# An rwkv chunk scan on one core: products half crossed and half straight over TensorE's four quadrants, in alternation; the chain of a unit spread over three steps, both directions in one eviction, the state carried in PSUM

## The reference, cut to what matters

```
def step(s, inp):
    rt, wt, kt, vt, at, bt = inp
    sa = jnp.einsum('bhij,bhj->bhi', s, at)
    s = s * wt[:, :, None, :] + sa[..., None] * bt[:, :, None, :] + vt[..., None] * kt[:, :, None, :]
    y = jnp.einsum('bhij,bhj->bhi', s, rt) if with_out else None
    return s, y
```

## Time and profile before

| what | value |
|---|---|
| median of 3 runs | 3626.92 us (3624.53 to 3631.20) |
| profiled execution, its own time | 3630.52 us |
| its span in the trace | 3628.7 us |
| mean granted TensorE clock | 0.968 |
| busy: TensorE matmul, VectorE, ScalarE, POOL | 3374.2, 1622.8, 1152.1, 403.9 us |
| the rwkv scan in the span | from about 1485 to 2258 us |

### The profile page before, as it was taken

How to read it: one execution, slowest core, us unless ns; L and a number is a source line. 1 busy time by engine, 2 the same in 40 slices (tenths; PEclk the granted TensorE clock), 3 DMA queues, 4 the chain that set the end, 5 groups by cost and what they waited for, 6 DMA issues and landing times. The chain is left out here.

```text
span 3628.7 us, 79113 instructions
## 1 busy us (share of the span) xinstructions
PE 3374.2 (93%) x35358; PEld 2634.2 (73%) x35358; DVE 1622.8 (45%) x3112; ACT 1152.1 (32%) x2433; POOL 403.9 (11%) x615
## 2 busy tenths in 40 slices
PE   7998998999999699899999999999989898899998
PEld 5767976788888568799999887788867676534343
DVE  3354455433333452367777675433344564211112
ACT  3343233322223332345555444322243333100001
POOL 0000122100000100222222221000011200100000
PEclk9999999999999899999999999999999999799999
DMA  4493153211111210000000001322111223499996
GB/s 184 141 357 126 47 226 117 93 70 47 70 70 52 85 47 24 9 6 6 5 13 5 28 5 41 121 97 93 70 68 51 81 76 139 208 403 411 414 428 289
DMA packets 35235, 437.39 MB, mean 121 GB/s; under 512 B 5024, under 2 KB 5632, under 8 KB 9168
## 3 DMA queue, kind: packets, MB, share of 16 engines
q1 hardware_dynamic: 29856, 414.10, 28.6%
q0 software_dynamic: 5040, 18.23, 1.6%
HBM read 425.49 MB, written 6.82 MB: 119 GB/s over the span
## 5 line engine op out<-in xcount | busy, mean ns | idle before, releaser
L758 PE MATMUL ps<-part 128*128 128x512 f32 (+1 forms) x4656 | 856.8, 346 | 43.4 <-DVE part L998 16.2
L758 PEld LDWEIGHTS ps<-part 128*128 128x128 f32 x4656 | 734.1, 194 | 162.3 <-issue 20.4
L2053 PE MATMUL ps<-part 128*128 128x512 f32 (+1 forms) x1536 | 549.3, 358 | 18.4 <-DVE part L2100 11.8
L2054 PE MATMUL ps<-part 128*128 128x512 f32 (+1 forms) x1536 | 548.6, 357 | 0.0
L2055 PE MATMUL ps<-part 128*128 128x512 f32 (+1 forms) x1536 | 548.4, 357 | 0.0
L3880 PE MATMUL ps<-part 128*64 128x512 f32 x1536 | 374.6, 608 | 27.9 <-DMA part<-in_wg 14.0
L2077 DVE TENSOR_TENSOR part<-part 128x1024 fp32r<-128x1024 f32 x128 | 158.7, 1240 | 495.3 <-ACT part L2066 495.3
L2477 PE MATMUL ps<-part 64*64 64x64 f32 x9984 | 340.6, 219 | 10.4 <-DVE part L2635 4.6
L2053 PEld LDWEIGHTS ps<-part 128*128 128x128 f32 x1536 | 289.8, 189 | 68.2 <-DVE part L2100 12.9
L2477 PEld LDWEIGHTS ps<-part 64*64 64x64 f32 x9984 | 315.5, 135 | 30.8 <-ACT part L2880 7.3
L2054 PEld LDWEIGHTS ps<-part 128*128 128x128 f32 x1536 | 290.3, 189 | 46.5
(11 more groups left out here) (419 smaller groups left out, 4320.4 us busy)
## 6 DMA issues: line engine op xcount, KB each, us to landing
part<-in_ada_w SPq DMA_DIRECT2D x36, 2048.0 KB, 9.6
part<-in_mlp_w SPq DMA_DIRECT2D x32, 2048.0 KB, 7.6
part<-in_wg SPq DMA_DIRECT2D x32, 2048.0 KB, 14.3
part<-in_wu SPq DMA_DIRECT2D x32, 2048.0 KB, 13.2
part<-in_wd SPq DMA_DIRECT2D x32, 2048.0 KB, 14.0
part<-in_b_in SPq DMA_DIRECT2D x8, 2048.0 KB, 7.5
part<-in_ab_w_in SPq DMA_DIRECT2D x7, 2048.0 KB, 8.0
part<-in_rkv SPq DMA_DIRECT2D x6, 2048.0 KB, 7.4
```

Of the source, the lines that this page charges most:

```text
L758: mm = pe.e.matmul(ps[:, j * n:j * n + n], lhs, rhs, start=k == ks[0] and i == 0, stop=k == ks[-1] and i == 2)
L2053: pe.e.matmul(ps, wh[:, k, :], hi[:, k, x0:x1], start=k == 0, stop=False)
L2054: pe.e.matmul(ps, wh[:, k, :], lo[:, k, x0:x1], start=False, stop=False)
```

## The change

The scan functions are written anew. Every engine now walks a clock (rw_clock), c from -2 to 25 with 12 turns each:

- **Crossed and straight.** Half of the kinds of products now write to the other half of the partitions (flip = 1: head 0 from partitions 0 to 63 to 64 to 127, head 1 the other way): gram, X turned, PX, XM, rh, uu and y. X add, the squares, bk, ka, XMT, br and zz stay straight. Two generators yield after each pair, and together() takes one pair from each in turn (one such step is a slot). The products of stream parts stand behind 4 to 12 empty steps in turns 1, 6, 8 and 10, in which only the straight generator gives a pair.
- **Three steps.** The chain of unit n stretches from c = n-1 (turns 4 to 11: gram, squares, two additions) over c = n (third addition, PX, XM, turnings, ka, br) to c = n+1 (stream). Prep stands two units ahead, in PREP_FIRST and PREP_LAST. Operands and X have 3 buffers, the small gains 4.
- **Joined evictions.** Both directions of X add, the third squares, X turned, PX, XM, XMT, br, rh, uu, zz and y have one bank; all but the copies of zz and y are evicted by one instruction (128 or 512 columns).
- **State in PSUM.** An identity product adds the old state in PSUM ahead of the v and uu products, and ScalarE copies the sum with the gain as its scale, once per direction. VectorE's update and POOL's scaling are gone.
- **XT** is kept up by a product of its own (XMT, M times XT; before in the bank of XM) and its own addition. **y** is kept with its halves swapped; two additions over 64 partitions each put them right in r.ys.

The diff, cut to its core:

```diff
 KEYS = {0: 0, 1: 1, 2: 2, 3: 3, 6: 4, 7: 5}
-PREP = {1: 0, 3: 1, 4: 2, 5: 3, 6: 4, 7: 5, 8: 6, 9: 7}
+PREP_FIRST = {4: 0, 6: 1, 8: 2, 9: 3, 11: 4}
+PREP_LAST = {0: 5, 1: 6, 2: 7}
 RW_GATES = {4: (0, 1), 5: (2, 3), 6: (4, 5), 7: (6, 7)}
-END = {TURNS: 0, TURNS + 2: 1, TURNS + 4: 2, TURNS + 6: 3, TURNS + 8: 4, TURNS + 10: 5}
+END = {0: 0, 2: 1, 4: 2, 6: 3, 8: 4, 10: 5}
...
+def rw_clock():
+
+    for c in range(-2, UNITS + 2):
         for turn in range(TURNS):
-            if (n < 0 or n % 3 == 1) and keys < 8 and turn in KEYS:
...
+def prep_at(c, turn):
+
+    if turn in PREP_FIRST and here(c + 2):
+        return PREP_FIRST[turn], c + 2
+    if turn in PREP_LAST and here(c + 1):
+        return PREP_LAST[turn], c + 1
+    return None, 0
...
+def together(*works):
+
+    works = list(works)
+    while works:
+        for work in list(works):
+            if next(work, "done") == "done":
+                works.remove(work)
...
+    def blocks(ps, o, lhs, rhs, flip, *done):
...
         for g in range(4):
             for hd, h in halves():
-                mm = pe.e.matmul(ps[h, o + g * 64:o + g * 64 + 64], lhs[h, g, :], rhs[h, g, :], start=True, stop=True)
...
+                mm = pe.e.matmul(ps[half(hd ^ flip), o + g * 64:o + g * 64 + 64], lhs[h, g, :], rhs[h, g, :], start=True,
+                                 stop=True)
+            if g == 3 and done:
+                mm.then_inc(*pe.up(*done))
+            yield
...
+    def right_hand(n, sub):
+
+        bank = K.bank("rh", n, sub)
+        for u in both(K, n):
+            g, cs, x = u.chunk(sub)
...
+            ps = bank[:, 64 * u.d:64 * u.d + 64]
+            pe.wait_ge(K.at("A", u.d, n), K.at("v rows", u.m))
+            for hd, o in halves():
+                mm = pe.e.matmul(ps[half(1 - hd)], u.A[o, g, 0, :], r.V[u.m % 2][o, x, :], start=True, stop=first,
+                                 skip_group_check=True)
+            yield
+            if not first:
+                pe.wait_ge(K.at("zm", n, sub))
+                for hd, o in halves():
+                    mm = pe.e.matmul(ps[half(1 - hd)], u.aa[o, cs], r.zm[sub % 2][o, u.d, :], start=False, stop=True,
+                                     skip_group_check=True)
+            if u.d:
+                mm.then_inc(*pe.up(("rh", n, sub)))
+            yield
+
+    def solution(n, sub):
...
+        pe.wait_ge(K.at("rh in", n, sub), K.at("X", n, 5))
+        bank = K.bank("uu", n, sub)
...
+            for hd, o in halves():
+                mm = pe.e.matmul(ps[half(1 - hd)], u.X[o, g, :], r.RH[o, u.d, :], start=True, stop=True)
+            if u.d:
+                mm.then_inc(*pe.up(("uu", n, sub)))
+            yield
...
+    def states(n, sub):
+
+        if not following(n, sub):
+            return
+        bank = K.bank("zz", n, sub)
+        pe.wait_ge(K.at("BK", n))
...
+            ps = bank[:, 64 * u.d:64 * u.d + 64]
+            if not first:
+                for hd, o in halves():
+                    pe.e.matmul(ps[o], K.ident[o, o], r.zm[sub % 2][o, u.d, :], start=True, stop=False, skip_group_check=True)
+                yield
+            for hd, o in halves():
+                pe.e.matmul(ps[o], u.BK[o, 1, g, :], r.V[u.m % 2][o, x, :], start=first, stop=False, skip_group_check=True)
+            yield
+            pe.wait_ge(K.at("uu in", n, sub))
+            for hd, o in halves():
+                mm = pe.e.matmul(ps[o], u.BK[o, 0, g, :], r.UU[sub % 2][o, u.d, :], start=False, stop=True,
+                                 skip_group_check=True)
+            if u.d:
+                mm.then_inc(*pe.up(("zz", n, sub), *streamed(n, sub)))
+            yield
...
+    def crossed(c, turn):
+
+        n = c + 1
+        if turn == 4 and here(n):
...
-                gram(u, ps[:, :, 1:2, :], u.aa, u.ops[:, 1:2, :])
-                gram(u, ps[:, :, 0:1, :], u.bb, u.ops[:, 0:1, :]).then_inc(*pe.up(("gram", *u.key)))
...
+                yield from gram(ps[:, :, 1:2, :], u, u.aa, u.ops[:, 1:2, :], 1)
+                yield from gram(ps[:, :, 0:1, :], u, u.bb, u.ops[:, 0:1, :], 1, ("gram", *u.key))
+        n = c
+        if turn == 3 and here(n):
...
+            ps = K.bank("X turned", n)
+            for u in both(K, n):
+                yield from turned(ps, 256 * u.d, [u.X[:, g, :] for g in range(4)], 1, *([("X turned", n)] if u.d else []))
+        if turn in (3, 7) and here(n):
...
+            ps = K.bank(("PX", lev), n)
+            for u in both(K, n):
+                yield from blocks(ps, 256 * u.d, u.Pf, u.X, 1, *([(("PX", lev), n)] if u.d else []))
+        if turn in (5, 9) and here(n):
+            lev = turn // 4
+            pe.wait_ge(K.at("M", n, lev), K.at("XT", n, lev))
+            ps = K.bank(("XM", lev), n)
...
+                yield from blocks(ps, 256 * u.d, u.XT, u.M, 1, *([(("XM", lev), n)] if u.d else []))
+        n = c - 1
+        if here(n):
+            for _ in range({1: 4, 6: 8, 8: 12, 10: 8}.get(turn, 0)):
+                yield
+            sub, part = divmod(turn, 3)
+            yield from (right_hand, solution, outputs)[part](n, sub)
+
+    def straight(c, turn):
...
+        n = c
+        if turn == 1 and here(n):
...
+            ps = K.bank(("X add", 2), n)
+            for u in both(K, n):
+                yield from blocks(ps, 256 * u.d, u.NP[:, 1], u.X, 0, *([(("X add", 2), n)] if u.d else []))
...
-                    mm = pe.e.matmul(ps[o, 0:64], u.XX[o, 0, g, :], rh[o, :], start=True, stop=True)
...
-                        for hd, o in halves():
-                            mm = pe.e.matmul(ps[o, 0:64], u.BK[o, k, g, :], w[o, :], start=k == 0, stop=k == 1,
...
-                            mm = pe.e.matmul(ps[o, 0:64], w[o, :], A[o, :], start=k == 0, stop=k == 2, skip_group_check=True)
...
+        together(crossed(c, turn), straight(c, turn))
...
+            v.wait_ge(v.now(), K.at(("X add", 2), n))
+            v.e.tensor_tensor(four(r.X[n % 3]), four(r.X[n % 3]), K.ps.of(("X add", 2), n), ADD).then_inc(
...
-            if to:
-                z, ps = s.zm[(sub + 1) % 2], K.ps.of("zz", *c)[:, 0:64]
-                gain = u.gain(sub + 1) if sub < 3 else Unit(K, u.d, u.n + 1).gain(0)
-                v.wait_ge(K.at("zz", *c), K.at("gain", *to[:2]))
-                if u.b or sub:
-                    v.wait_ge(K.at("zm scaled", *c))
-                    inst = v.e.scalar_tensor_tensor(out=z, in0=ps, scalar=gain, in1=s.zg, op0=MUL, op1=ADD)
...
-                inst.then_inc(*v.up(("zm", *to), free("zz", *c)))
...
+            for hd, o in halves():
+                v.e.tensor_tensor(ys[o, :], y0[half(1 - hd), :], y1[half(1 - hd), :], ADD).then_inc(*v.up(("y sum", m)))
...
+    for c, turn in rw_clock():
+        n = c - 1
+        if here(n):
+            sub, part = divmod(turn, 3)
+            to = following(n, sub)
+            if part == 0:
+                s.wait_ge(K.at("rh", n, sub), K.at("uu", *previous(n, sub)) if n or sub else {})
+                s.e.activation(r.RH.rearrange("p d c -> p (d c)"), K.ps.of("rh", n, sub)[:, 0:128], ACT.Copy).then_inc(
+                    *s.up(("rh in", n, sub), free("rh", n, sub)))
+            if part == 1:
...
+                s.e.activation(r.UU[sub % 2].rearrange("p d c -> p (d c)"), K.ps.of("uu", n, sub)[:, 0:128],
+                               ACT.Copy).then_inc(*s.up(("uu in", n, sub), free("uu", n, sub)))
+            if part == 2 and to:
...
+                for u, w in zip(both(K, n), both(K, to[0])):
+                    s.wait_ge(K.at("gain", *w.key))
+                    s.e.activation(r.zm[to[1] % 2][:, u.d, :], K.ps.of("zz", n, sub)[:, 64 * u.d:64 * u.d + 64], ACT.Copy,
+                                   scale=w.gain(to[1])).then_inc(*s.up(("zm", *to), free("zz", n, sub)))
...
-        if what == "stream" and turn % 3 == 0:
...
-                pool.e.tensor_tensor(s.zg, s.zm[sub % 2], gain.to_broadcast([128, 64]), MUL).then_inc(
-                    *pool.up(("zm scaled", *c)))
```

More of the change, by code:

```diff
@@ new lines, in straight @@
+                    yield from turned(ps, 256 * i, [w[:, u.toks[it][j]] for it in range(2) for j in range(2)], 0,
+                                      *([("bk", *u.key)] if i else []))
+        if turn == 4 and here(n):
+            for u in both(K, n):
+                ps = K.bank("ka", *u.key).rearrange("p (g x c) -> p g x c", g=4, x=2)
+                to = slice(0, 4, 3) if u.lat else slice(0, 1)
+                yield from gram(ps[:, :, 0:2 if u.lat else 1, :], u, u.ks, u.ops[:, to, :], 0, ("ka", *u.key))
@@ new lines, in straight @@
+        if turn == 5 and here(n):
+            ps = K.bank("XMT", n)
+            pe.wait_ge(K.at("M", n, 1), K.at("XT", n, 1))
+            for u in both(K, n):
+                yield from blocks(ps, 256 * u.d, u.M, u.XT, 0, *([("XMT", n)] if u.d else []))
+        if turn == 7 and here(n) and n % 3:
+            ps = K.bank("br", n).rearrange("p (d g x c) -> p d g x c", d=2, g=4, x=1)
+            for u in both(K, n):
```

(14 more changed lines are left out.)

825 lines of the change are left out of this document (398 added, 427 removed).

## The result

The changed kernel takes **3651.85 us** (median of 4 runs, 3650.32 to 3652.69) against 3628.30 before (4 runs on the same chip): ratio **1.0059**, 95% interval [1.0044, 1.0073], 23.6 us slower. The forecast was 3560, faster. The time lies inside the stated range and on the other side of no change.

What follows compares the result with a forecast made beforehand. The scan was taken as bound by TensorE's matmul rate (97% busy). 23.3 us plus 4.3 of waits gave 27.6 us a period against 30.6, 69 us less over 23 periods: 3560 us, own range 3515 to 3605, whole range 3480 to 3670.

Steps and rivals of the forecast that it cites:

- I therefore price a slot with a crossed and a straight pair at 117 ns: TensorE in the scan: one step of together() with two pairs costs 117 ns, as with one; bounds 117 and 234.
- the issue floor: Rival, 9%: matmul starts at least about 25 ns apart make two-pair slots 200 ns; 37 us slower, 3667.
- no overlap: Rival, 7%: column halves do not overlap at 64 columns, 234 ns a two-pair slot; 78 us slower, 3709.
- 23.3 us per period before any wait: TensorE in the scan: slots, wide products, turned v and gates sum to 69.8 us per group of three periods.
- That makes 2.7: Scan: TensorE's new waits for late evictions, summed by turns, are 2.7 us a period.
- 4.3 us per period: Scan: TensorE's whole waits, the 2.7 us of new ones plus today's 1.6 us of restarts and queueing.
- Turns 1, 2 and 11: Scan: waits of 0.7 us from turn 11 to 0, 0.2 in turn 1, 0.7 to 0.8 in turn 2.
- the zm copies stand behind two Pf copies and four tanh: 0.8: Turn 6 of the scan: TensorE waits 0.8 us a period for zm copies queued on ScalarE.
- Neither binds. POOL loses its state scaling, off the path: Other engines in the scan: VectorE at 55 of the new 83 us and ScalarE do not limit.
- The clock: TensorE's clock in the scan: read as full, 1.00, before the change.
- I count nothing; bounds 5 us less, 10 more: Scan's head and end: extra period at the head, BK eight turns earlier; net zero counted, within those bounds.
- Waits take over: Rival, 12%: late evictions stop both sides; decides from 7.3 us of waits a period; at 8.5, 28 us slower, 3658.

Runs made afterwards that it cites:

- x7: Changed kernel with the edits of x3 and x5, VectorE's ka mask moved from turn 6 to turn 4, and k-sum scaling moved to ScalarE: 3571.47 us.
- x3: Changed kernel with ScalarE running the four tanh ahead of the UU and Pf copies in turn 4: 3618.54 us.
- x1: Changed kernel with the product kk raw moved from VectorE to ScalarE: 3647.96 us.
- x2: Changed kernel with the kk product kept on VectorE but issued five turns earlier: 3654.40 us.
- x5: Changed kernel with all steps per pair of heads issued three to four turns later, behind POOL's chain: 3632.35 us.
- x13: x7 with an increment of a spare semaphore on TensorE's queue before each pair of gram, blocks and turned: 3901.09 us.
- x14: The kernel before the change with the same semaphore increments as x13: 3878.17 us.

## Why the prediction was wrong

- **"I therefore price a slot with a crossed and a straight pair at 117 ns": right.** 116 ns. The two rivals on the array fall: the issue floor (200 ns) and no overlap (234). The rule of the Trainium skill that was weighed there (TensorE: Matmul & The Clock Gate, about 25 ns from start to start) does not hold across quadrants: 14.5 ns.
- **"23.3 us per period before any wait": right as the array's time, but hardly to be kept up.** x7 has matmuls in flight for 23.8 us a period. (The sum takes the latent unit's pairs for all three; its 160 slots hold for the context unit too, its 232 pairs do not: there they are 200. The two rivals on the array are priced too dear by it.) But the array was taken as the only limit of TensorE. Of the gaps between 1525 and 2160 us, 42 of 128 us end behind an instruction block in the changed kernel, and 78 of 89 in x7. The changed kernel has 881 records a period (20638 in 728 us, 31.1 us each). In 23.3 us that is 26.4 ns a record, the best pace of loading seen (3.3 us a block is 26 ns) and beyond its median (3.8, 30 ns).
- **"That makes 2.7", and with it "4.3 us per period": the failed step.** TensorE is idle 6.4 us a period, and the places are other ones. That is 2.1 of the 3.5 us by which the period of 31.1 misses 27.6; the other 1.4 are busy time, 24.7 against 23.3, and the slow clock below can account for up to 1.2 of them. Turns 1, 2 and 11 (UU and zm copies), for which 1.6 us was counted, cost 0.7. Turn 6's "the zm copies stand behind two Pf copies and four tanh: 0.8" names the right instruction and the wrong wait: TensorE stops in turn 5, for the PSUM bank that tanh frees, 43.5 us in all (1.8 a period; x3). The ring of banks stood in no step of the working. Nor did the mask of ka (22 us with the part before rh).
- **"Neither binds. POOL loses its state scaling, off the path": wrong.** POOL's products of two units now run back to back in turns 0 to 2, beside VectorE's steps per pair of heads, and hold them 5.4 us each (x1, x2, x5). That made 27.6 us of TensorE's waits, and one POOL product held VectorE 4.1 us at the scan's end. By busy time alone the sentence holds: VectorE has 61 us per group of three periods, 5.4 of them the held product, where 55 were forecast. No row of before shows it, since there the steps did not meet.
- **The clock** was taken at 1.00 throughout, as in the earlier trace rows. It is granted 1.2 GHz in or just behind stops of 3 us (tanh) and 3 to 5 us (kk); one was of 8.9. Matmuls are in flight for 57 of the 73 us, and at most half of that is lost, 28 us, 1.2 a period; x7, without the long stops, reads 1.00 in its group of 90 us. No run changes the clock alone.
- **Head and end**, "I count nothing; bounds 5 us less, 10 more": 4.8 less and 12.1 more up to the end of the stream, 7.3 in all. With the 5.9 of the last norm and gate it is 13.2, outside the bounds; 4.1 of the 5.9 are VectorE beside POOL. It should have been counted.
- **The rival "Waits take over"** was the case (31.1 us a period where it decides from 30.6, and 3651.85 where it gave 3658), at 12%. That its number is so near is in part luck: the waits are 6.4 us a period, below the 7.3 from which it was to decide, and busy time, in part of slow clock, makes up the rest. Its place was half right: not the chain behind the RH copy, but banks, ports and loading.

With the order put right (x7) the forecast's own numbers appear: 27.9 us a period against 27.6, 3571 against 3560. The array's part of it is the forecast's; that the idle time, 4.1 us a period, comes out at the forecast's 4.3 is luck, for 3.4 of it are gaps behind instruction blocks and not evictions.

**Open:** why VectorE gets no turn between POOL's instructions in six cases and got one in another; what fixes the 3.3 us from block to block; why TensorE stops at blocks in x13 and x14, where they are 5.4 us apart; and the 11 of 89 us of x7's gaps that do not follow a block.

## What to carry to other kernels

When an engine has been the bound at 97%, list what else it needs besides its array before pricing a faster one: banks in their ring order with the engine that frees each, and instructions per microsecond. Moving steps in an order by hand can set VectorE's fp32 instructions from SBUF to SBUF beside POOL's; look in the trace for one that lasts many times its median, and move the whole group away, since moving one only passes the stall on. After a long idle stretch, count the slow clock too.

## What the runs showed of the hardware

- Crossed and straight pairs of 64 x 64 fp32 products run side by side at 14.5 ns a record (64 records in 0.93 us).
- A VectorE instruction beside back-to-back POOL products took 6.00 to 6.13 us instead of 0.61 in six cases of eight. With it moved away, another took its place: a y addition (6.04 instead of 0.69) or the aa x kk product (4.18 instead of 0.71).
- TensorE's instructions come in DMAs of 16 KB, one for 127.5 matmul records, at best every 3.3 us; with 128 records of 64 columns to a block that is nearly the pace of two quadrants (29.2 ns), and half that of four.
- An increment of a semaphore on TensorE's queue added 68 to 87 ns to the time (x14, x13).
